# Entry work between the chunks of the last two input slots, and one of four probability tiles scaled on VectorE

## The chip, the cores and the metric

One NeuronCore of a Trainium2 chip runs the kernel. The time is that of the device, in microseconds from the start of the program to its end, taken as the median of several executions. A granted TensorE clock of 1.00 is 2.4 GHz and one of 0.50 is 1.2 GHz.

## The reference, cut to what matters

The program is a stack of two "first" layers (a feed-forward, a mixer with latent attention and convolution, a second feed-forward, a gated embedding) and then one "second" block. The change lies in the mixer of the second block, for 512 tokens and a width of 1024:

```python
z = h @ w_in                                  # 19 slots of 128 columns here
g_rnn, x_rnn, q, k_c, v_c, k_s, v_s, k_w, v_w, gate_logits = jnp.split(z, splits, axis=-1)
...
kc = compress_blocks(to_heads(k_c), ...)      # 31 compressed blocks of keys, and vc of values
...
p_c = jax.nn.softmax(sc, axis=-1) * ...       # scores against the 31 blocks
o_c = jnp.einsum('bgrqc,bgcd->bgrqd', p_c, vc)
...
p_s = jax.nn.softmax(ss...)                   # all blocks are selected at 512 tokens
o_s = jnp.einsum('bgrqnk,bgqnkd->bgrqd', p_s, v_sel)
...
o_w = jnp.einsum('bgrqk,bgkd->bgrqd', jax.nn.softmax(sw, axis=-1), vwb)
return gb[0] * o_c + gb[1] * o_s + gb[2] * o_w
```

So there are three attentions with a common query: one against 31 compressed blocks, and two (called `s` and `w`) that are causal over the tokens. Each is multiplied by a gate, and the gate is folded into the reciprocal of the softmax sum. The multiplication of the probabilities by that number is what the change divides between two engines.

## The kernel before, in words

Everything is fp32, each large product made of three matmuls of split operands (a high and a low part each). The engines run in parallel from orders written out by hand, one straight list for each engine, and meet at counting semaphores. TensorE is called PE, VectorE DVE, ScalarE ACT and GpSimd POOL.

**Input slots.** A weight slot is 128 output columns by the full depth of 1024. `slot_mm` (L1132) works through its 8 chunks of depth (k = 0 to 7), 3 matmuls each, into one of 4 PSUM banks `proj[0..3]`, slot number modulo 4. DVE then takes the bank out (L2054 for slots 15 to 18, which are the queries). DVE also makes the low part of the weights of a slot two slots ahead (L1581, `w_lo`), after ACT has made the high part (L652). Slot 18 is the last.

**Entry.** Between slots 17 and 18 PE does the entry work of the attention (L1428 to L1455): 8 transposes of the two value tensors into `sc` (L1433), 2 of the compressed hidden layer (L1438), the first score pair `scores2(0, 0)` (L1351), the compressed keys and values (L1445 and L1450) and `scores2(0, 1)`. On DVE the partners of these stand in the iteration for slot 17: the hidden layer (L2105, L2106), the gates (L2110), the copies of the turned values (L2115), the hidden columns (L2117), then the first softmax step. After slot 18 come `scores2(1, ...)` and `compressed()` (L1331, 32 matmuls of only 31 columns), which needs slot 18's queries.

**Steps.** The attention has 16 steps g. Four steps make one head pair: 128 queries each, against 512, 384, 256 and 128 keys. A step has four score tiles i (two attentions by two head groups). DVE takes the scores from PSUM, adds the bias and finds the maximum in `biased(g, i)` (L1991); ACT exponentiates and sums (L914); `gated(g)` on DVE makes the reciprocal (L1997) and multiplies it by the gate (L2000); POOL multiplies the four probability tiles by it in `scale(g)` (L623); PE turns them three steps later (`turn2`, L1362) into three PSUM banks in rotation; ACT and DVE take turns at copying these out (`copy_2`, L992 and L2168). So a turn needs the copy of the turn three before it. After four steps `values` (L1375, L1380) multiplies a head pair's turned probabilities by the values, and `take2` on DVE (L2172) copies the result.

**The low parts of the recurrent branch** (`u_lo`, L2179, 4 tiles) stand on DVE between `gated(1)` and the compressed scores. Their reader is the output projection (L1487) after the attention.

## Time and profile before

| | us |
|---|---|
| median of 3 runs | 3057.77 (3054.81 to 3058.88) |
| the profiled execution | 3060.09, span 3058.3 |
| mean granted TensorE clock over the span | 0.989 |
| PE busy | 3001.4 (98%) |
| DVE, ACT, POOL busy | 1699.3, 1109.3, 319.0 |

The span is cut by the profiler from the first to the last instruction; the time of an execution holds some 1.8 us more. Busy times of PE come from pipelined matmuls with modelled ends, so PE can read as busy while it goes at half its clock or below its best rate. The stage that the change touches lies between 2527 and 2639 us from the start.

### The profile page before, as it was taken

To read this page: it belongs to the slowest core of one execution; us is meant where nothing else is said; L and a number is where in the kernel's file an instruction comes from. 1 tells how busy PE (TensorE), PEld (TensorE's weight loads), DVE (VectorE), ACT (ScalarE), POOL (GpSimd) and SP (SyncE) were. 2 spreads that over 40 slices of the span, in tenths; PEclk is the share of its full clock that TensorE was granted. 3 is DMA by queue.
4 is the path that set the end of the run, shared out by engine and by line. 5 is a ranking of instruction groups with operands and counts; after the bars stand their busy time and mean duration, and the time that the engine had idled before them with its cause. 6 is when DMAs were issued, how large, how long until landed. Compare 5 with 4: busy or idle time off the path is not lost. (4 is left out here: it accounts for less than half of the span.)

```text
span 3058.3 us, 37437 instructions
## 1 busy us (share of the span) xinstructions
PE 3001.4 (98%) x13534; PEld 2437.9 (80%) x13534; DVE 1699.3 (56%) x2387; ACT 1109.3 (36%) x1724; POOL 319.0 (10%) x254
## 2 busy tenths in 40 slices
PE   7999999999999999999999999999999999989999
PEld 6888888778888887888888888888888775678887
DVE  6555565565654556555456455655546677453334
ACT  4222333562332234322232454332324555552223
POOL 1000200000100024000030000200003216500000
PEclk9999999999999999999999999999999998999999
DMA  5242222123323222432222212343222420122222
GB/s 186 87 151 96 90 96 83 57 61 114 138 96 144 97 79 94 147 138 100 91 99 92 84 37 88 107 144 138 97 93 83 158 76 22 42 70 97 96 96 82
DMA packets 86809, 301.58 MB, mean 99 GB/s; under 512 B 10272, under 2 KB 19616, under 8 KB 85536
## 3 DMA queue, kind: packets, MB, share of 16 engines
q1 hardware_dynamic: 86688, 300.02, 28.6%
q8 instruction: 70, 1.15, 0.1%
q14 instruction: 51, 0.42, 0.0%
HBM read 297.88 MB, written 2.10 MB: 98 GB/s over the span
## 5 line engine op out<-in xcount | busy, mean ns | idle before, releaser
L1128 PE MATMUL proj<-u_hi,w_hi 128*128 128x512 f32 x2616 | 1029.9, 394 | 28.3 <-DVE u_lo L1586 22.0
L1130 PE MATMUL proj<-u_hi,w_lo 128*128 128x512 f32 x2616 | 1021.8, 391 | 0.0
L1129 PE MATMUL proj<-u_lo,w_hi 128*128 128x512 f32 x2616 | 1021.6, 391 | 0.0
L1581 DVE TENSOR_TENSOR w_lo<-raw,w_hi 128x1024 fp32r<-128x1024 f32 (+4 forms) x567 | 656.7, 1161 | 492.6 <-ACT w_hi L652 483.2
L652 ACT ACTIVATE w_hi<-raw 128x1024 fp32r<-128x1024 f32 (+4 forms) x567 | 536.2, 954 | 342.2 <-PE proj L1130 220.3
L1128 PEld LDWEIGHTS proj<-u_hi,w_hi 128*128 128x128 f32 x2616 | 493.0, 188 | 141.5 <-issue 23.5
L1129 PEld LDWEIGHTS proj<-u_lo,w_hi 128*128 128x128 f32 x2616 | 493.2, 189 | 103.4 <-issue 2.9
L1130 PEld LDWEIGHTS proj<-u_hi,w_lo 128*128 128x128 f32 x2616 | 492.8, 188 | 103.2
L1128 PE MATMUL proj<-a_hi,w_hi 128*128 128x512 f32 x936 | 368.4, 394 | 3.1 <-DVE w_lo L1581 1.5
L1130 PE MATMUL proj<-a_hi,w_lo 128*128 128x512 f32 x936 | 365.2, 390 | 0.0
L1129 PE MATMUL proj<-a_lo,w_hi 128*128 128x512 f32 x936 | 364.8, 390 | 0.0
L1597 DVE TENSOR_TENSOR work<-proj,rs 128x512 f32<-128x512 f32 x260 | 179.4, 690 | 286.8 <-PE proj L1130 286.6
L694 ACT ACTIVATE a_hi<-work 128x512 f32 (+1 forms) x88 | 55.6, 632 | 441.3 <-DVE work L1652 441.3
L1128 PEld LDWEIGHTS proj<-a_hi,w_hi 128*128 128x128 f32 x936 | 175.9, 188 | 42.1 <-DVE a_lo L1655 2.6
L1130 PEld LDWEIGHTS proj<-a_hi,w_lo 128*128 128x128 f32 x936 | 175.7, 188 | 37.1
L1129 PEld LDWEIGHTS proj<-a_lo,w_hi 128*128 128x128 f32 x936 | 176.0, 188 | 34.3
L549 POOL TENSOR_TENSOR acc<-h 128x512 f32<-128x512 f32 x6 | 6.2, 1040 | 1519.3 <-DVE h L1670 1320.1
L1670 DVE SCALAR_TENSOR_TENSOR h<-proj,h 128x512 f32<-128x512 f32 x96 | 66.3, 691 | 165.8 <-PE proj L1130 165.7
L691 ACT ACTIVATE work<-work 128x512 f32<-128x512 f32 x88 | 55.6, 632 | 267.7 <-DVE work L1597 267.7
L1655 DVE TENSOR_TENSOR a_lo<-work,a_hi 128x512 f32 (+1 forms) x88 | 61.0, 693 | 80.4 <-ACT a_hi L694 80.4
L658 ACT ACTIVATE u_hi<-h,vec 128x512 fp32r<-128x512 f32 x48 | 34.8, 724 | 141.1 <-DVE h L1670 82.2
L552 POOL TENSOR_TENSOR sq<-h 128x512 f32<-128x512 f32 x42 | 62.1, 1478 | 72.5 <-DVE h L1918 40.0
(459 smaller groups left out, 2922.4 us busy)
## 6 DMA issues: line engine op xcount, KB each, us to landing
raw<-in_ffn_gu SPq DMA_DIRECT2D x174, 512.0 KB, 3.3
raw<-in_in_w SPq DMA_DIRECT2D x68, 512.0 KB, 3.2
raw<-in_ffn_dn SPq DMA_DIRECT2D x64, 512.0 KB, 3.2
raw<-in_ff SPq DMA_DIRECT2D x64, 512.0 KB, 3.3
gate<-in_ada SPq DMA_DIRECT2D x8, 3072.0 KB, 11.4
raw<-in_ffn_dn SPq DMA_DIRECT2D x32, 384.0 KB, 3.0
raw<-in_in SPq DMA_DIRECT2D x18, 512.0 KB, 3.4
raw<-in_mla_out SPq DMA_DIRECT2D x16, 512.0 KB, 3.3
```

Source lines behind the costliest of these rows:

```text
L552: pool.tensor_tensor(sq, x(m), x(m), ALU.mult).then_inc(sq_ready, 1)
L652: act.activation(wt(w_hi, slot, slot.tiles), wt(raw, slot, slot.tiles), ACT.Copy)\
L658: act.activation(u_hi(m), h(m), ACT.Copy, scale=gain[:, m:m + 1]).then_inc(u_hi_ready, 1)
L691: act.activation(work(2 + q), work(q), ACT.Tanh, scale=0.5).then_inc(tanh_ready, 1)
L694: act.activation(a_hi_t[:, bass.ds((2 * it + q) * S, S)], work(8 + q), ACT.Copy)\
L1128: pe.matmul(out, w_h, x_h, start=first, stop=False)
L1129: pe.matmul(out, w_h, x_l, start=False, stop=False)
L1130: return pe.matmul(out, w_l, x_h, start=False, stop=last)
L1581: dve.tensor_tensor(wt(w_lo, slot, slot.tiles), wt(raw, slot, slot.tiles), wt(w_hi, slot, slot.tiles).bitcast(F32), ALU.subtract).then_inc ...
L1597: return dve.tensor_tensor(dst, proj[:, slot.pos, :], rs, ALU.mult)
L1655: dve.tensor_tensor(a_lo_t[:, at], work(8 + q), a_hi_t[:, at].bitcast(F32), ALU.subtract)\
L1670: dve.scalar_tensor_tensor(at, proj[:, slot.pos, :], 0.25, at, ALU.mult, ALU.add)\
```

## The change

PE's entry work goes between the chunks of slots 17 and 18: at chunk 3 of slot 17 the 8 transposes, now into the banks `proj[3]` and `proj[0]`; at chunk 4 of slot 18 the first score pair and the 2 transposes; at chunk 6 the compressed keys and values and the second score pair. DVE's copies of the turned values move ahead of taking out slot 17. In each step DVE scales tile 0 itself, right behind `gated`, and POOL the other three; the one counter `p2_ready` becomes `p2_pool` and `p2_dve`. The four `u_lo` tiles move from behind `gated(1)` to the loop pass g = 16 (STEPS), ahead of a `take2` and of the last copies.

```diff
--- before.py
+++ after.py
@@ -255,8 +255,9 @@
         dist_ready, hid_part = sem("dist_ready"), sem("hid_part")
         cs_done, cs_exp, pc_step, pc_ready = (sem(n) for n in ("cs_done", "cs_exp", "pc_step", "pc_ready"))
         cs_sub = sem("cs_sub")
-        s2_done, max2, exp2, inv2 = sem("s2_done"), sem("max2"), sem("exp2"), sem("inv2")
-        ginv2, p2_ready, t2_done, o2_done, o2_ready = (sem(n) for n in ("ginv2", "p2_ready", "t2_done", "o2_done", "o2_ready"))
+        s2_done, max2, exp2 = sem("s2_done"), sem("max2"), sem("exp2")
+        ginv2, t2_done, o2_done, o2_ready = (sem(n) for n in ("ginv2", "t2_done", "o2_done", "o2_ready"))
+        p2_pool, p2_dve = sem("p2_pool"), sem("p2_dve")
         pt_act, pt_dve = sem("pt_act"), sem("pt_dve")
         h_turned, h_copied, h_sized = sem("h_turned"), sem("h_copied"), sem("h_sized")
         gain_diag, gain_rows = sem("gain_diag"), sem("gain_rows")
@@ -362,6 +363,7 @@
         t_bank = lambda n: (tr[:, :], proj[:, 2, :], proj[:, 3, :])[n % 3]
         turn_no = lambda g, i: 4 * g + i + (2 if g >= 2 else 0)
         TURN_C = 8
+        scaled = lambda g, i: (p2_pool, 3 * g + i) if i else (p2_dve, g + 1)
         by_act = lambda n: n % 2 == 0
         copied = lambda n: (pt_act if by_act(n) else pt_dve, n // 2 + 1)
 
@@ -619,8 +621,8 @@
             def scale(g):
 
                 pool.wait_ge(ginv2, g + 1)
-                for i in range(4):
-                    pool.tensor_scalar(prob(g, i), prob(g, i), esum(g, i), None, ALU.mult).then_inc(p2_ready, 1)
+                for i in range(1, 4):
+                    pool.tensor_scalar(prob(g, i), prob(g, i), esum(g, i), None, ALU.mult).then_inc(p2_pool, 1)
 
             for g in range(2):
                 scale(g)
@@ -1353,7 +1355,7 @@
 
             def turn2(g, i):
                 n = turn_no(g, i)
-                pe.wait_ge(p2_ready, 4 * g + i + 1)
+                pe.wait_ge(*scaled(g, i))
                 if n >= 3:
                     pe.wait_ge(*copied(n - 3))
                 elif n:
@@ -1382,11 +1384,46 @@
                         if br and k == QT - 1:
                             mm.then_inc(o2_done, 1)
 
+            def beside_17(k):
+
+                if k == 3:
+                    pe.wait_ge(slot_read, Slot(L2, 16).done)
+                    for bank, v in ((3, VS), (0, VW)):
+                        for t in range(QT):
+                            mm = pe.transpose(proj[:, bank, t * P:(t + 1) * P], v[:, t * P:(t + 1) * P], ident[:, :])
+                        mm.then_inc(v2_turned, 1)
+
+            def beside_18(k):
+
+                if k == 4:
+                    pe.wait_ge(h_copied, KD + 3)
+                    scores2(0, 0)
+                    pe.wait_ge(hid_ready, 1)
+                    pe.wait_ge(g_cols, 1)
+                    for m in range(2):
+                        mm = pe.transpose(tr[:, m * P:(m + 1) * P], hid_x[:, m * P:(m + 1) * P], ident[:, :])
+                    mm.then_inc(hid_turned, 1)
+                if k == 6:
+                    pe.wait_ge(hid_cols, 1)
+                    pe.wait_ge(v2_copied, 2)
+                    for m in range(2):
+                        pe.matmul(tr[:, 0:62], w2k(m), hid(0, m), start=m == 0, stop=m == 1)
+                    for g in range(2):
+                        for m in range(2):
+
+                            for c in range(0, P, 32):
+                                mm = pe.matmul(proj[c:c + N_CMP, 3, g * 64:(g + 1) * 64],
+                                               hid(1, m)[:, g * N_CMP:(g + 1) * N_CMP], w2v(m),
+                                               start=m == 0 and g == 0, stop=m == 1, skip_group_check=True)
+                    mm.then_inc(kv_cmp_done, 1)
+                    pe.wait_ge(slot_read, Slot(L2, 17).done)
+                    scores2(0, 1)
+
             for s in range(IN2):
                 if s == 0:
                     two_slots((Slot(L2, 0), Slot(L2, 1)), u_of, lambda k: pe.wait_ge(u_ready, 8 * KD + k + 1))
                 elif s > 1:
-                    slot_mm(Slot(L2, s), u_of)
+                    slot_mm(Slot(L2, s), u_of, {17: beside_17, 18: beside_18}.get(s))
                 if 5 <= s <= 8:
 
                     j = s - 5
@@ -1425,35 +1462,6 @@
                     for t in range(QT):
                         mm = pe.transpose(tr[:, t * P:(t + 1) * P], gT[:, t * P:(t + 1) * P], ident[:, :])
                     mm.then_inc(g_turned, 1)
-                if s == 17:
-
-                    pe.wait_ge(h_copied, KD + 3)
-                    for i, v in enumerate((VS, VW)):
-                        for t in range(QT):
-                            mm = pe.transpose(sc[:, i, t * P:(t + 1) * P], v[:, t * P:(t + 1) * P], ident[:, :])
-                        mm.then_inc(v2_turned, 1)
-                    pe.wait_ge(hid_ready, 1)
-                    pe.wait_ge(g_cols, 1)
-                    for m in range(2):
-                        mm = pe.transpose(tr[:, m * P:(m + 1) * P], hid_x[:, m * P:(m + 1) * P], ident[:, :])
-                    mm.then_inc(hid_turned, 1)
-                    pe.wait_ge(slot_read, Slot(L2, 15).done)
-                    pe.wait_ge(v2_copied, 2)
-                    scores2(0, 0)
-                    pe.wait_ge(hid_cols, 1)
-                    for m in range(2):
-                        pe.matmul(tr[:, 0:62], w2k(m), hid(0, m), start=m == 0, stop=m == 1)
-                    for g in range(2):
-                        for m in range(2):
-
-                            for c in range(0, P, 32):
-                                mm = pe.matmul(proj[c:c + N_CMP, 3, g * 64:(g + 1) * 64],
-                                               hid(1, m)[:, g * N_CMP:(g + 1) * N_CMP], w2v(m),
-                                               start=m == 0 and g == 0, stop=m == 1, skip_group_check=True)
-                    mm.then_inc(kv_cmp_done, 1)
-                    pe.wait_ge(slot_read, Slot(L2, 17).done)
-                    scores2(0, 1)
-
             scores2(1, 0)
             scores2(1, 1)
             compressed()
@@ -1994,10 +2002,11 @@
             def gated(g):
                 j, qt, w = step(g)
                 dve.wait_ge(exp2, 4 * g + 4)
-                dve.reciprocal(esum(g, 0, 4), esum(g, 0, 4)).then_inc(inv2, 1)
-                dve.wait_ge(inv2, g + 1)
+                link(dve.reciprocal(esum(g, 0, 4), esum(g, 0, 4)))
                 inv = esum(g, 0, 4).rearrange("p (b g) -> p b g", b=2)
                 dve.tensor_tensor(inv, inv, gates4[:, qt, 1:3, :, j], ALU.mult).then_inc(ginv2, 1)
+                dve.wait_ge(ginv2, g + 1)
+                dve.tensor_scalar(prob(g, 0), prob(g, 0), esum(g, 0), None, ALU.mult).then_inc(p2_dve, 1)
 
             def build_blocks(kv, g):
 
@@ -2049,6 +2058,10 @@
                     link(dve.scalar_tensor_tensor(top, poly, 2.0, top, ALU.mult, ALU.add))
 
                     link(dve.tensor_scalar(small2[:, 0:4], top, -4.0, None, ALU.mult))
+                if s == 17:
+                    for i, d in enumerate((vn_s, vn_w)):
+                        dve.wait_ge(v2_turned, i + 1)
+                        dve.tensor_copy(d, proj[:, (3, 0)[i], :]).then_inc(v2_copied, 1)
                 if 15 <= s:
                     dve.wait_ge(slot_done, slot.done)
                     dve.scalar_tensor_tensor(dst[s], proj[:, slot.pos, :], q_scale[:, s - 15:s - 14], rs, ALU.mult, ALU.mult)\
@@ -2110,9 +2123,6 @@
                     dve.tensor_scalar(gcols.rearrange("p (t c) -> p t c", t=QT),
                                       tr[:, :].rearrange("p (t c) -> p t c", t=QT)[:, :, 0:24],
                                       1.0, 0.5, ALU.add, ALU.mult).then_inc(g_cols, 1)
-                    for i, d in enumerate((vn_s, vn_w)):
-                        dve.wait_ge(v2_turned, i + 1)
-                        dve.tensor_copy(d, sc[:, i, :]).then_inc(v2_copied, 1)
                     dve.wait_ge(hid_turned, 1)
                     dve.tensor_copy(hid_c, tr[:, 0:2 * P]).then_inc(hid_cols, 1)
                     dve.wait_ge(dist_ready, 2)
@@ -2174,10 +2184,6 @@
             for i in range(4):
                 biased(1, i)
             gated(1)
-            for j in range(4):
-                dve.wait_ge(u_hi_ready, 9 * KD + j + 1)
-                dve.scalar_tensor_tensor(u_lo(j), gr(j), c2(C_RNN + j), u_hi(j).bitcast(F32), ALU.mult, ALU.subtract)\
-                   .then_inc(u_ready, 1)
             cmp_scores()
             for g in range(2, STEPS + 3):
                 behind = g - 2 if g < 4 else g - 3 if g >= 5 else None
@@ -2193,6 +2199,10 @@
                     biased(g, 3)
                 if behind is not None:
                     copy_2(behind, 3)
+                for j in range(4) if g == STEPS else ():
+                    dve.wait_ge(u_hi_ready, 9 * KD + j + 1)
+                    dve.scalar_tensor_tensor(u_lo(j), gr(j), c2(C_RNN + j), u_hi(j).bitcast(F32), ALU.mult, ALU.subtract)\
+                       .then_inc(u_ready, 1)
                 if g == 2:
                     cmp_norm()
                 if g == 4:
```

PE around slots 17 and 18, in the order of before (`sc`, `tr`, `proj` are PSUM; `ax` holds queries, keys and values; the three rows L1128 to L1130 are one chunk): the entry stands in one piece between two slots.

```order
L1130 MATMUL proj<-u_hi,w_lo 128x512
L1433 MATMUL sc<-ident,ax 128x128 [waits h_copied]
L1433 MATMUL sc<-ident,ax 128x128 x7
L1438 MATMUL tr<-ident,ax 128x128 [waits g_cols,hid_ready]
L1438 MATMUL tr<-ident,ax 128x128
L1351 MATMUL sc<-ax 128x512 [waits v2_copied,slot_read]
L1351 MATMUL sc<-ax 128x512
L1445 MATMUL tr<-acc,sq 128x62 [waits hid_cols]
L1445 MATMUL tr<-acc,sq 128x62
L1450 MATMUL proj<-sq,acc 31x64 x16
L1351 MATMUL proj<-ax 128x512 [waits slot_read]
L1351 MATMUL proj<-ax 128x512
```

PE in the changed kernel, inside slot 18, from the last matmul of chunk 3 on:

```order
L1132 MATMUL proj<-u_hi,w_lo 128x512
L1353 MATMUL sc<-ax 128x512 [waits h_copied]
L1353 MATMUL sc<-ax 128x512
L1404 MATMUL tr<-ident,ax 128x128 [waits g_cols,hid_ready]
L1404 MATMUL tr<-ident,ax 128x128
L1130 MATMUL proj<-u_hi,w_hi 128x512
L1131 MATMUL proj<-u_lo,w_hi 128x512
L1132 MATMUL proj<-u_hi,w_lo 128x512
```

The waits are the same, but chunks of slot 18 now stand ahead of them and between them.

DVE at the end of the attention, before (`gate` takes the turned probabilities; the row of L2172 is `take2(2)`, the two of 2x128 are the copies of step 14):

```order
L1997 RECIPROCAL row_stats<-row_stats 128x4 [waits exp2]
L2000 TENSOR_TENSOR row_stats<-row_stats,rope_table 128x4 [waits inv2]
L2168 COPY gate<-proj 128x3x128 [waits t2_done]
L2168 COPY gate<-tr 128x3x128 [waits t2_done]
L2172 COPY work<-ot 128x512 [waits o2_done]
L2168 COPY gate<-proj 128x2x128 [waits t2_done] x2
```

DVE at the same place in the changed kernel:

```order
L2005 RECIPROCAL row_stats<-row_stats 128x4 [waits exp2]
L2007 TENSOR_TENSOR row_stats<-row_stats,rope_table 128x4 [waits start_step]
L2009 TENSOR_SCALAR work<-work,row_stats 128x128 [waits ginv2]
L2178 COPY gate<-proj 128x3x128 [waits t2_done]
L2178 COPY gate<-tr 128x3x128 [waits t2_done]
L2204 SCALAR_TENSOR_TENSOR u_lo<-ax,col_76,u_hi 128x512 [waits u_hi_ready] x4
L2182 COPY work<-ot 128x512 [waits o2_done]
L2178 COPY gate<-proj 128x2x128 [waits t2_done] x2
```

The four `u_lo` tiles came in ahead of `take2(2)` and of the copies of step 14, and one scale came in behind the product with the gates.

## Rows read from the trace of the kernel before

**Rows 1.** Engines and granted clock by stretch; columns: us, then busy time of each.

```profile
core 0: us, PE busy (x) PEld busy (x) DVE busy (x) ACT busy (x) POOL busy (x), PEclk, DMA share, GB/s
2536.50:2543.30 6.80, 6.01 (x46) 2.81 (x44) 2.42 (x7) 1.52 (x4) 0.00 (x0) 0.50 0.01 2
2553.70:2570.60 16.90, 14.87 (x62) 10.08 (x60) 16.27 (x42) 11.30 (x37) 12.66 (x10) 0.50 0.00 0
2615.10:2621.80 6.70, 6.70 (x25) 2.83 (x22) 0.90 (x7) 0.88 (x4) 6.70 (x6) 0.50 0.00 0
2632.20:2635.50 3.30, 3.30 (x14) 1.28 (x12) 0.00 (x0) 0.00 (x0) 0.00 (x0) 0.50 0.00 0
```

**Rows 2.** Timeline of PE around the entry: start, us, instruction, idle before.

```profile
2527.33 0.48 PE L1128 MATMUL proj<-u_hi,w_hi 128*128 128x512 f32 x1
...
2532.91 1.03 PE L1433 MATMUL sc<-ident,ax 128*128 128x128 f32 x8
2536.22 0.41 PE L1438 MATMUL tr<-ident,ax 128*128 128x128 f32 x2 [2.28 <-DVE rope_table L2110]
2537.42 2.08 PE L1351 MATMUL sc<-ax 64*128 64x512 f32 x4 [0.79 <-DVE ax L2115]
2539.43 1.11 PE L1445 MATMUL tr<-acc,sq 128*128 128x62 f32 x4
...
2541.48 2.04 PE L1351 MATMUL proj<-ax 64*128 64x512 f32 x4
...
2549.13 0.92 PE L1351 MATMUL sc<-ax 64*128 64x384 f32 x4
...
2550.53 4.09 PE L1331 MATMUL proj<-rope_table,ax 64*128 64x31 f32 x64
```

**Rows 3.** Timeline of DVE over the same stretch.

```profile
2533.11 0.75 DVE L2054 SCALAR_TENSOR_TENSOR ax<-proj,q_scale,rs 128x512 f32<-128x512 f32 x1 [0.21 <-PE proj L1130]
...
2536.00 1.28 DVE L2115 COPY ax<-sc 128x512 f32<-128x512 f32 x2
...
2543.55 0.69 DVE L1991 CUSTOM_DVE_ANT_0 work<-proj,work 128x512 f32<-128x512 f32 x1 [2.60 <-PE proj L1351]
...
2546.79 1.29 DVE L1581 TENSOR_TENSOR w_lo<-raw,w_hi 128x1024 fp32r<-128x1024 f32 x1 [0.57 <-ACT w_hi L652]
2549.24 0.75 DVE L2054 SCALAR_TENSOR_TENSOR ax<-proj,q_scale,rs 128x512 f32<-128x512 f32 x1 [1.16 <-PE proj L1130]
...
2553.91 3.29 DVE L2179 SCALAR_TENSOR_TENSOR u_lo<-ax,col,u_hi 128x512 fp32r<-128x512 f32 x4 [0.24 <-ACT u_hi L1002]
2557.13 1.24 DVE L2134 TENSOR_TENSOR ux<-proj,work 128x496 f32<-128x496 f32 x2
```

**Rows 4.** The matmuls of L1331 alone, 0.4 us at each clock.

```profile
2552.40:2552.80 0.40, 0.40 (x12) 0.40 (x10) 1.00 0.00 0
2554.00:2554.40 0.40, 0.40 (x6) 0.40 (x6) 0.50 0.00 0
```

**Rows 5.** Groups of DVE, the same scaling in the first attention: busy, mean ns.

```profile
L1749 DVE TENSOR_SCALAR work<-work,row_stats 128x512 f32<-128x512 f32 x16 | 7.8, 486 | 0.6
L1749 DVE TENSOR_SCALAR work<-work,row_stats 128x384 f32<-128x384 f32 x16 | 6.7, 420 | 0.6
...
L1749 DVE TENSOR_SCALAR work<-work,row_stats 128x128 f32<-128x128 f32 x16 | 4.6, 287 | 0.6
```

**Rows 6.** Timeline of POOL, the starts of two successive head pairs.

```profile
2593.31 12.88 POOL L623 TENSOR_SCALAR work<-work,row_stats 128x512 f32<-128x512 f32 x10 [1.65 <-DVE row_stats L2000]
...
2611.64 12.88 POOL L623 TENSOR_SCALAR work<-work,row_stats 128x512 f32<-128x512 f32 x10 [1.33 <-DVE row_stats L2000]
```

**Rows 7.** Engines in steps 8 to 10, columns as in Rows 1.

```profile
2587.60:2597.30 9.70, 9.37 (x52) 4.71 (x52) 9.57 (x41) 8.84 (x29) 7.94 (x9) 1.00 0.01 3
```

**Rows 8.** Timeline of PE and of DVE at the end of the attention.

```profile
2629.75 0.30 PE L1362 MATMUL proj<-ident,work 128*128 128x128 f32 x1 [0.30 <-DVE gate L2168]
...
2631.80 6.22 PE L1380 MATMUL ot<-gate,ax 128*64 128x512 f32 x32
...
2641.31 2.74 DVE L2212 SCALAR_TENSOR_TENSOR u_lo<-work,col,u_hi 128x512 fp32r<-128x512 f32 x4 [2.53 <-ACT u_hi L1030]
```

## The prediction

> **What bounds the kernel now.** I cut the stretch from 2527 to 2639 us by granted clock first. Four stretches stand at 0.50, which is 1.2 GHz: 6.8, 16.9, 6.7 and 3.3 us long [rows 1]. The first follows a wait of PE, the second follows the compressed scores, the third the thin steps of a head pair, the fourth the last turns. So in this stage a wait costs its length and may cost half of what PE does afterwards.
>
> Next the timeline of PE. Between slots 17 and 18 it runs the entry from 2532.91 and waits 2.28 us for the gates and 0.79 us for the turned values; what follows goes at half clock until about 2543.3. The scores of step 1 start at 2549.13, which is the end of slot 18 [rows 1, 2]. Next the timeline of DVE: it takes out slot 18 at 2549.24, then spends 3.29 us on `u_lo` from 2553.91, so that the compressed scores, which PE has ready at about 2554.6, are taken up only at 2557.13 [rows 2, 3]. Until the end of that stretch at half clock DVE is busy 16.27 of 16.90 us [rows 1] and sets the pace, whatever the clock of PE.
>
> In the later head pairs PE and DVE are both nearly full: 9.37 and 9.57 of 9.70 us in steps 8 to 10 [rows 7]. POOL has 17.0 us of work in each 18.33 us (from 2593.31 to 2611.64, of which it idled 1.33 [rows 6]). It is close to being the bound, but it waits for DVE and not the reverse, and its results are used three steps later.
>
> **Entry on PE.** Slot 17 starts at 2527.33 and takes 5.58 us without the transposes [rows 2]. These read 1.03 us busy, with the overlap at both ends about 0.9, so slot 18 starts at 2533.8. Four chunks are half of 5.5 us: 2536.5. The first score pair took 2.0 at half clock from 2537.42 to 2539.43 [rows 2]; at full clock 1.1, with 0.3 for the two transposes: 2537.9. Does it wait? The transposes wait for the gates, which came 3.1 us after DVE began to take out slot 17 (2533.11 to 2536.22 [rows 2, 3]). Now the two value copies, 1.28 us [rows 3], go ahead of that, from 2533.0 on, so slot 17 is taken out at 2534.2 and the gates are there at 2537.3, before the 2537.6 at which PE asks. The margin is 0.3 us; without it the wait is tenths. Chunks 4 and 5 take 1.4, compressed keys and values 1.0 (2.05 at half clock, 2539.43 to 2541.48), the second score pair 1.1, chunks 6 and 7 1.4: slot 18 ends at about 2543.0 instead of 2549.1. **PE gains 6.1 us there**, about 3.1 in waits and 3 in clock. The entry's new waits stand in front of chunks, but nothing queued behind them is due earlier.
>
> **What of it arrives.** DVE's string from the second score pair to the low weights ran from 2543.55 to 2546.79 [rows 3]. It now starts near 2541.7, so the low weights of slot 20 start at 2544.9, behind the new 0.486 us scale [rows 5], which fits ahead of that; slot 18 is taken out at 2546.2 and its queries are there at 2547.0. PE has then finished the scores of step 1 (1.4 us before, 2549.13 to 2550.53 [rows 2]) since about 2544.6 and waits 2.4 us. That is a new wait as long as the one removed. `compressed()` takes 3.9 us at full clock. Its rate is 12 records in 0.4 us at full clock and 6 at half [rows 4]; the clock fell during it even with no wait before it. With a 2.4 us wait in front I expect the fall inside it, somewhere between 2547 and 2550.4, by the nearest case, the wait of rows 2 where the clock was down 0.3 us after it. So it ends between 2551.5 and 2554.9; I take 2553.2. DVE starts there instead of at 2557.13 because `u_lo` is gone: **gain 3.9 us** (2.2 to 5.6; 6.1 if the clock holds). From here DVE's work sets the pace and carries the gain, less the scale of step 2, 0.4 us (between rows 5's 384 and 128 forms). The return of the clock at 2570.6 may come later relative to the work: 0 to 1.7, I take 0 in the likeliest case.
>
> The page "TensorE: Matmul & The Clock Gate" of the Trainium skill, section "Why this matters for your kernels", blames idle gaps between bursts of matmuls for a fall of the clock. The first fall agrees. The second does not: PE went from the scores at 2549.13 straight into the compressed ones and lost the clock within them [rows 1, 2]. By the rule alone, the thin steps of rival B below would be safe; by the row they are not.
>
> **The scale on DVE.** DVE has the same operation in the first attention at 486, 420 and 287 ns [rows 5]. In a head pair the scales of 128, 512 and 384 columns (those behind `gated` of steps 4m-1, 4m, 4m+1) fall where DVE has 0.13 us of idle in 9.7 [rows 7]: 0.29 + 0.49 + 0.42 = 1.2 us. The fourth falls while PE multiplies the values, when DVE is idle (0.90 busy of 6.7 us in the third stretch [rows 1]). PE is nearly full too, so a little slack is eaten: about 1.0 for each of steps 8 to 10 and 12 to 14, and 0.5 for steps 4 to 6, where DVE waits a little. **Loss 2.5 us** (0.5 to 3.6). POOL loses a quarter of 17.0 us in each head pair, which nobody waits for: 0.
>
> "GPSIMD Engine Reference" of the Trainium skill, section "Key points", says that POOL and VectorE contend for shared SBUF interfaces, in VectorE's two-port modes or with two SBUF inputs. The trace agrees for the latter: four `u_lo` tiles took 3.29 us beside busy POOL and the four of L2212 2.74 beside an idle one [rows 3, 8]. By that ratio, 1.2, the scales would cost 0.2 us more in a head pair.
>
> **The tail.** DVE has at g = 16: the copies of step 13, then `u_lo` x4, `take2(2)`, the copies of step 14. PE's turns of step 15 need the copy of (14, 1); before, PE was already released by a DVE copy there, at 2629.75 after 0.30 us of waiting [rows 8]. So there is no slack: POOL is nearly done, u_lo costs 2.7 us by the row of L2212 [rows 8] to 3.3 [rows 3], and step 15's scale 0.3 sits ahead of it. **Loss 2.9 us** (2.7 to 3.6; nothing if the copies turned out to wait for PE anyway). The last 32 value matmuls took 6.22 us with 3.3 us of half clock inside [rows 1, 8], so about 4.7 at full. After a wait near 3 us they may run almost wholly at half clock: +0.9 (0 to +3). The third stretch at half clock, 6.7 us, costs half of itself, 3.4; it came in one of three head pairs. I leave it in, and it may vanish or double.
>
> **Sum**, against the execution profiled (span 3058.3, its own time 3060.1): -3.9 + 0.4 + 2.5 + 2.9 + 0.9 = +2.8, so 3062.9. That execution lay 2.3 above the median of the three runs, 3057.8; on that footing the forecast is 3060.6, and I give **3060.5 us**.
>
> **Rivals.** What a measurement can tell from no change is 0.2%, 6.1 us: 3051.7 to 3063.9.
> - *A. The entry's gain is spent again by the new DVE work and the tail* (the forecast): 3052 to 3064. Chance 0.58.
> - *B. Slower: the clock.* The added DVE work thins PE's steps, and one more head pair falls to 1.2 GHz: 3060.5 + 3.4, with the late return of the clock (+1.7) about 3065.6. For it: steps 12 to 14 fell with PE waiting only tenths, and a little more idling comes to each pair. It decides once one fall more than before comes. Chance 0.22.
> - *C. Faster: POOL was the late one.* Then three tiles instead of four let PE's turns start earlier, the scales on DVE hide, and the `u_lo` tiles find idle DVE: -3.9 - 3.4 (no third fall) with losses of 0.5 near the tail: about 3051. For it: POOL is 93% busy. Against it: it waits 1.3 to 1.65 us for DVE in each pair, and the end of the turns is released by a DVE copy. Chance 0.15.
> - *D. The clock holds through the compressed scores* and the rest is as in A: 3060.5 - 2.2 = 3058.3. Chance 0.05.
>
> **Range.** 3052 to 3067: from the early end of A with the third fall gone (3060.5 - 1.7 - 1.5 - 3.4 - 0.9 is 3053, and C lies just beyond), to B with the full tail price. By 0.2%: faster 0.18 (C and a little of A), same 0.60, slower 0.22.
>
> **What would show it.** In the new profile: PE without a wait between slots 17 and 18 and slot 18 done 6 us sooner; then a wait of about 2.4 us ahead of the compressed scores, and their rate halving within; DVE at L2144 3 to 5 us earlier; two starts of POOL's 512-column group some 19 us apart instead of 18.3; PE waiting about 3 us for a DVE copy in the last turns. The forecast fails if the copies of step 14 had slack, if DVE was not the pace of steps 8 to 14, or if the falls of the clock come at other places.

## The result, and the profile after

| | median us | range | executions |
|---|---|---|---|
| before | 3056.43 | 3053.78 to 3058.88 | 8 |
| changed | 3064.80 | 3061.01 to 3067.06 | 8 |

The ratio is 1.0025, interval 1.0017 to 1.0034: slower by 5.2 to 10.4 us, most likely 7.6. That is just beyond the 0.2% (6.1 us) under which the forecast counts two times as the same; its figure was 3060.5 and its range ended at 3067. Every execution of the changed kernel was slower than the slowest of before. Of the executions of before that ran beside the experiments below, one stood apart at 3749.35 us with a granted clock of 0.754 and is not counted.

The profiled execution of the changed kernel took 3061.01, 3.8 below its median; that of before took 3060.09, 3.7 above its own. Side by side the two profiles show 1 us and not 8. So the traces are read for the place and the size of each step, and the medians for the sum.

First the page's totals, as the busy times of before stand in its table; then the engines by stretch, columns as in [rows 1].

```profile
span 3059.3 us, 37437 instructions
PE 2999.9 (98%) x13534; PEld 2433.9 (80%) x13534; DVE 1705.7 (56%) x2403; ACT 1109.9 (36%) x1724; POOL 303.9 (10%) x238
```

```profile
core 0: us, PE busy (x) PEld busy (x) DVE busy (x) ACT busy (x) POOL busy (x), PEclk, DMA share, GB/s
2549.20:2556.00 6.80, 6.80 (x42) 5.17 (x41) 5.53 (x10) 5.41 (x11) 5.75 (x5) 0.51 0.00 1
2562.80:2569.70 6.90, 6.67 (x21) 3.47 (x20) 5.40 (x21) 4.60 (x14) 4.24 (x6) 0.52 0.01 2
2593.50:2600.40 6.90, 6.89 (x24) 2.63 (x25) 2.28 (x12) 1.12 (x5) 6.90 (x7) 0.52 0.00 0
2631.10:2637.90 6.80, 6.72 (x23) 2.56 (x25) 0.36 (x2) 0.27 (x1) 0.00 (x0) 0.51 0.01 2
2583.80:2593.50 9.70, 8.75 (x48) 4.72 (x46) 9.49 (x36) 8.30 (x26) 5.70 (x6) 1.00 0.01 3
```

Sixteen scales went from POOL (319.0 to 303.9 us) to DVE (1699.3 to 1705.7). The stage has 27.4 us at half clock here, where before had 33.7 [rows 1]: this execution is not slower because the clock fell more. The last row begins in the same step as [rows 7] and is as long: DVE is as full as it was (9.49 of 9.70 us), while PE fell from 9.37 to 8.75. PE now waits for DVE there.

The timeline of PE, at the entry, in the second head pair and in the tail:

```profile
2536.09 1.13 PE L1353 MATMUL sc<-ax 64*128 64x512 f32 x4
...
2542.53 0.92 PE L1353 MATMUL sc<-ax 64*128 64x384 f32 x4
...
2546.66 4.60 PE L1333 MATMUL proj<-rope_table,ax 64*128 64x31 f32 x64 [2.57 <-DVE ax L2067]
...
2574.41 1.07 PE L1377 MATMUL ot<-ux,rope_table 31*64 31x512 f32 x4 [0.26 <-DVE gate L2178]
...
2590.56 0.30 PE L1364 MATMUL tr<-ident,work 128*128 128x128 f32 x1 [0.54 <-DVE gate L2178]
...
2593.51 1.77 PE L1377 MATMUL ot<-ux,rope_table 31*64 31x512 f32 x4 [0.25 <-DVE gate L2178]
...
2630.42 0.30 PE L1364 MATMUL proj<-ident,work 128*128 128x128 f32 x1 [2.69 <-DVE gate L2178]
...
2631.45 1.97 PE L1377 MATMUL ot<-ux,rope_table 31*64 31x512 f32 x4
2633.36 6.87 PE L1382 MATMUL ot<-gate,ax 128*64 128x512 f32 x32
```

The entry has no wait. Slot 18 is done at 2542.53, where it was 2549.13 [rows 2]; slot 17 began 0.5 sooner in this execution, so 6.1 of the 6.6 are the change's. The compressed scores wait 2.57 us for slot 18's queries (L2067). The tail has a wait of 2.69 us for a copy of DVE where before had 0.30 [rows 8]. The half clock from 2593.50 takes the place of that from 2615.10 before [rows 1], one head pair earlier.

The timeline of DVE, entry and tail:

```profile
2532.30 1.28 DVE L2064 COPY ax<-proj 128x512 f32<-128x512 f32 x2
2533.50 0.74 DVE L2067 SCALAR_TENSOR_TENSOR ax<-proj,q_scale,rs 128x512 f32<-128x512 f32 x1
...
2536.23 0.23 DVE L2123 TENSOR_SCALAR rope_table<-tr 128x96 f32<-128x96 f32 x1
...
2545.78 0.74 DVE L2067 SCALAR_TENSOR_TENSOR ax<-proj,q_scale,rs 128x512 f32<-128x512 f32 x1
...
2551.23 1.26 DVE L2144 TENSOR_TENSOR ux<-proj,work 128x496 f32<-128x496 f32 x2 [0.76 <-PE proj L1333]
...
2625.44 0.29 DVE L2009 TENSOR_SCALAR work<-work,row_stats 128x128 f32<-128x128 f32 x1
...
2626.58 2.76 DVE L2204 SCALAR_TENSOR_TENSOR u_lo<-ax,col,u_hi 128x512 fp32r<-128x512 f32 x4
...
2629.86 0.74 DVE L2178 COPY gate<-proj 128x256 f32<-128x256 f32 x2
```

The compressed scores are taken up (L2144) at 2551.23, where it was 2557.13 [rows 3]: 5.9 sooner, 5.4 without the offset. In the tail the four low parts stand between the copies of step 13 and that of step 14 for which PE waits.

DVE at the end of step 9, first in the kernel before and then in the changed one:

```profile
2595.65 0.17 DVE L2000 TENSOR_TENSOR row_stats<-row_stats,rope_table 128x4 f32<-128x4 f32 x1
2595.73 0.28 DVE L2168 COPY gate<-proj 128x128 f32<-128x128 f32 x1
```

```profile
2592.51 0.17 DVE L2007 TENSOR_TENSOR row_stats<-row_stats,rope_table 128x4 f32<-128x4 f32 x1
2592.71 0.55 DVE L2009 TENSOR_SCALAR work<-work,row_stats 128x384 f32<-128x384 f32 x1
2593.18 0.27 DVE L2178 COPY gate<-proj 128x128 f32<-128x128 f32 x1
```

The copy comes 0.67 us behind the start of the product with the gates, where it came 0.08. The scale takes 0.47 of that, by its start and the next one; the rest it waits for the product, whose counter it needs. In steps 7 and 8 the copy comes 0.40 and 0.60 behind, where it came 0.09 and 0.08. So the three scales cost DVE 1.42 us in a head pair, 1.07 of them the scales themselves.

POOL, for [rows 6], and the new scales on DVE by form, for [rows 5]:

```profile
2589.65 9.61 POOL L625 TENSOR_SCALAR work<-work,row_stats 128x512 f32<-128x512 f32 x7 [2.46 <-DVE row_stats L2007]
...
2612.03 9.62 POOL L625 TENSOR_SCALAR work<-work,row_stats 128x512 f32<-128x512 f32 x7 [2.46 <-DVE row_stats L2007]
```

```profile
L2009 DVE TENSOR_SCALAR work<-work,row_stats 128x256 f32<-128x256 f32 x4 | 2.4, 598 | 0.1
L2009 DVE TENSOR_SCALAR work<-work,row_stats 128x384 f32<-128x384 f32 x4 | 2.1, 520 | 0.1
L2009 DVE TENSOR_SCALAR work<-work,row_stats 128x512 f32<-128x512 f32 x4 | 1.9, 486 | 0.1
...
L2009 DVE TENSOR_SCALAR work<-work,row_stats 128x128 f32<-128x128 f32 x4 | 1.1, 286 | 0.1
```

POOL waits for DVE longer than before, 2.46 us against 1.33 to 1.65, and the timeline of PE shows no wait for POOL in this stage. Its two starts are 22.38 us apart and not some 19, because the half clock from 2593.50 lies between them; without half of its 6.9 us it would be 18.9.

In the kernel before, POOL was late once:

```profile
2574.19 0.41 PE L1362 MATMUL proj<-ident,work 128*128 128x128 f32 x2 [0.74 <-POOL ax L623]
```

With three tiles on POOL (the kernel with the scale alone, below) PE waits 0.99 us at that place, for ACT. So the relief of POOL brought nothing there, and rival C falls.

### The profile page after: what moved, and what is told of

Its sections match the earlier page's. It is cut to its first block and busy times, and to the rows that moved or that the text cites. A ratio compares the mean times of both kernels' runs of the same rounds, so it can differ in the third digit from the quotient of the medians.

```text
span 3059.3 us, 37437 instructions
## 1 busy us (share of the span) xinstructions
PE 2999.9 (98%) x13534; PEld 2433.9 (80%) x13534; DVE 1705.7 (56%) x2403; ACT 1109.9 (36%) x1724; POOL 303.9 (10%) x238
## 5 line engine op out<-in xcount | busy, mean ns | idle before, releaser
L1130 PE MATMUL proj<-u_hi,w_hi 128*128 128x512 f32 x2616 | 1029.3, 393 | 27.3 <-DVE u_lo L1594 20.9
L1130 PEld LDWEIGHTS proj<-u_hi,w_hi 128*128 128x128 f32 x2616 | 492.5, 188 | 140.8 <-issue 22.8
L1131 PEld LDWEIGHTS proj<-u_lo,w_hi 128*128 128x128 f32 x2616 | 493.0, 188 | 103.4 <-issue 2.9
L1130 PE MATMUL proj<-a_hi,w_hi 128*128 128x512 f32 x936 | 368.1, 393 | 3.1 <-DVE w_lo L1589 1.5
L1130 PEld LDWEIGHTS proj<-a_hi,w_hi 128*128 128x128 f32 x936 | 175.8, 188 | 42.1 <-DVE a_lo L1663 2.6
```

Of the source, the lines that this page charges most:

```text
L1130: pe.matmul(out, w_h, x_h, start=first, stop=False)
L1131: pe.matmul(out, w_h, x_l, start=False, stop=False)
```

## Experiments

"Stage" is read from each profile: from the start of slot 17 on PE to the first matmul behind the value matmuls (L1504, before L1496). It is 110.6 us before and 113.4 in the changed kernel. An execution that was early or late when the stage began does not disturb it, but the falls of the clock that this one execution had are in it. Ratios are to before on the same chip, with 11 executions of each kernel and 33 of before. A difference in us is the ratio's; where times fall into groups it can lie some us off that of the medians.

| kernel | median us | ratio, interval | profiled | stage |
|---|---|---|---|---|
| entry alone | 3055.63 | 1.0001 (0.9992 to 1.0010) | 3060.49 | 110.8 |
| scale on DVE alone | 3061.16 | 1.0016 (1.0007 to 1.0025) | 3063.19 | 113.5 |
| low parts moved, alone | 3058.61 | 1.0010 (1.0001 to 1.0019) | 3059.23 | 110.3 |
| changed, low parts back | 3059.52 | 1.0011 (1.0002 to 1.0020) | 3059.52 | 110.1 |
| changed, low parts behind the last copies | 3058.12 | 1.0007 (0.9998 to 1.0016) | 3057.95 | 109.4 |
| entry, low parts behind the last copies | 3055.28 | 0.9997 (0.9988 to 1.0006) | 3057.08 | 107.1 |
| the same, slot 18 out early | 3052.40 | 0.9995 (0.9986 to 1.0004) | 3051.07 | 101.5 |
| one scale in four on DVE | 3053.58 | 0.9986 (0.9977 to 0.9995) | 3048.39 | 100.0 |

**The entry alone.** Of the changed kernel, undone are the move of the low parts and the scale:

```diff
-                for i in range(1, 4):
+                for i in range(4):
                     pool.tensor_scalar(prob(g, i), prob(g, i), esum(g, i), None, ALU.mult).then_inc(p2_pool, 1)
...
             gated(1)
+            for j in range(4):
...
+                dve.scalar_tensor_tensor(u_lo(j), gr(j), c2(C_RNN + j), u_hi(j).bitcast(F32), ALU.mult, ALU.subtract)\
             cmp_scores()
```

> The entry between the chunks alone: POOL scales all four tiles and u_lo stands behind gated(1) as before. My sum: slot 18 done 6 us sooner, but the compressed scores wait some 2.5 us for slot 18's queries and DVE has u_lo in front of them, so DVE takes up the compressed scores 3.5 us sooner than before: about -3.5 us against the kernel before (range -6 to -1). Rival (clock): the new wait moves the fall of the clock into PE-bound work and the entry is worth nothing: 0 or above. Rival (pure gain): -6.

No change, with at most 2.4 us gained by the interval, where 3.5 was expected: a miss. Eight executions lie between 3053.97 and 3055.87 and three between 3060.07 and 3060.49; the profiled one is of the three. The timeline of PE in it:

```profile
2547.17 7.04 PE L1333 MATMUL proj<-rope_table,ax 64*128 64x31 f32 x64 [2.29 <-DVE ax L2065]
```

The compressed scores run wholly at half clock behind their new wait, 7.04 us, where the changed kernel's profile has 4.60 and before 4.09 [rows 2]. In this execution the wait and the clock together take back 2.29 + 2.95 us of what the entry won. The eight faster ones have no trace; their median lies only 1.2 below that of before.

**The scale alone.** In the kernel before:

```diff
-                for i in range(4):
-                    pool.tensor_scalar(prob(g, i), prob(g, i), esum(g, i), None, ALU.mult).then_inc(p2_ready, 1)
+                for i in range(1, 4):
+                    pool.tensor_scalar(prob(g, i), prob(g, i), esum(g, i), None, ALU.mult).then_inc(p2_pool, 1)
...
                 dve.tensor_tensor(inv, inv, gates4[:, qt, 1:3, :, j], ALU.mult).then_inc(ginv2, 1)
+                dve.wait_ge(ginv2, g + 1)
+                dve.tensor_scalar(prob(g, 0), prob(g, 0), esum(g, 0), None, ALU.mult).then_inc(p2_dve, 1)
```

> The first tile's scale on DVE alone, entry and u_lo as before. My sum: +2.9 us (0.4 for step 2, 0.5 and twice 1.0 for the three full head pairs, 0.3 at the end), so +1 to +4. Rival (clock): thinner steps let one more head pair fall to 1.2 GHz in most executions: +6. Rival (POOL was the late one): -1 or below.

Slower by 4.9 us (2.1 to 7.6). PE in its second head pair:

```profile
2580.49 1.07 PE L1377 MATMUL ot<-ux,rope_table 31*64 31x512 f32 x4
2596.65 0.30 PE L1364 MATMUL tr<-ident,work 128*128 128x128 f32 x1 [0.54 <-DVE gate L2171]
...
2599.60 1.94 PE L1377 MATMUL ot<-ux,rope_table 31*64 31x512 f32 x4 [0.26 <-DVE gate L2171]
```

From one value group to the next it takes 19.11 us, where before took 17.93 (2578.39 to 2596.32). The waits of the changed kernel, 0.54 and 0.26 us, are in it, so they come from the scale alone. The forecast's 2.9 lies inside the interval.

**The move of the low parts alone.** In the kernel before, the loop is taken from behind `gated(1)` and put behind `copy_2(behind, 3)` for `g == STEPS`, as in the change's diff.

> The move of the four u_lo tiles to the pass g = 16 alone. My sum: DVE takes up the compressed scores as soon as PE has them, 2.5 us sooner; the last turns wait 2.7 us for the copies of step 14 and the value matmuls after it go longer at half clock, 0.9: about +1.1 us (range -1 to +4). Rival (the tail costs more): the wait in the tail and the clock after it cost 6: +3.5. Rival (the tail is covered): -2.5.

Slower by 3.1 us (0.3 to 5.8), where 1.1 was expected and 3.5 by the rival of a dearer tail. PE and DVE in the tail:

```profile
2627.47 0.30 PE L1362 MATMUL proj<-ident,work 128*128 128x128 f32 x1 [3.02 <-DVE gate L2168]
```

```profile
2622.94 3.45 DVE L2194 SCALAR_TENSOR_TENSOR u_lo<-ax,col,u_hi 128x512 fp32r<-128x512 f32 x4
```

The wait of the tail comes from this part by itself. The three parts alone give +0.3, +4.9 and +3.1, which is 8.3 against the 7.6 of the whole: within their intervals, some 2.7 us either way each, they add up.

**The low parts put back in the changed kernel:** the second half of the diff of the entry alone.

> The changed kernel with u_lo back behind gated(1). The changed kernel measured +8 us against before. My sum: -3.5 for the entry, +2.9 for the scale: -0.6 (range -3 to +3), so the u_lo move would be what makes the changed kernel slower by most of 8. Rival (scale and clock): +4 to +6, nearly as slow as the changed kernel.

Slower than before by 3.4 us (0.6 to 6.1), 4.3 less than the changed kernel. The 0.6 faster that was expected missed by 4.0; the entry alone missed by 3.8. The prediction priced the tail, with its clock, at 3.8; the 4.3 is net of what the low parts cost DVE at the front, where they stand again.

**The low parts behind the last copies:**

```diff
-                for j in range(4) if g == STEPS else ():
+                for j in range(4) if g == STEPS + 2 else ():
```

> The changed kernel with the four u_lo tiles two passes later (g = 18), behind the last copies, where DVE idled 7 us. The changed kernel was +8 against before. If the tail is what u_lo costs there (wait of 2.7 us and half clock after it), this gives back 4 to 5 us: about +3.5 (range +2 to +5). Rival (a wait in the tail is no loss, the rest is clock chance elsewhere): stays above +6.

2.1 us slower than before (-0.6 to 4.9), so this one line gives back 5.5 of 7.6. No wait above 0.30 is left in its tail.

**The entry, with the low parts behind the last copies and four tiles on POOL:**

> Entry between the chunks, u_lo behind the last copies, POOL scales all four tiles. By adding the parts: entry 0, u_lo out of the front -2 to -3 and nothing in the tail, no scale on DVE: -3 (range -5 to 0) against before. Rival (POOL with four tiles becomes the bound once the front is shorter): 0 or above.

0.9 us faster than before (3.7 faster to 1.8 slower), not to be told from it; 3 was expected. Beside the last three kernels it gave 0.9995 (below). Against the kernel above, the scale makes 3.0 of difference.

**The same, slot 18 taken out early,** ahead of `gated(0)` and of the splitting of slot 20's weights:

```diff
                     dve.tensor_copy(vcmp, proj[:, 3, 0:P]).then_inc(kv_cmp_ready, 1)
+                    last = Slot(L2, 18)
+                    dve.wait_ge(slot_done, last.done)
+                    dve.scalar_tensor_tensor(dst[18], proj[:, last.pos, :], q_scale[:, 3:4], rs, ALU.mult, ALU.mult)\
+                       .then_inc(slot_read, 1)
                     gated(0)
```

> As the entry with u_lo at the end and POOL scaling four tiles, and DVE takes slot 18 out ahead of gated(0) and of the split of slot 20. If the wait ahead of the compressed scores (2.3 to 2.6 us) is what eats the entry's gain, by its length and by the clock in those scores (7.0 us instead of 3.9 where it fell at once), it shrinks to under 1 us here and the kernel gains 2 to 5 us more: -5 to -8 against before. Rival (DVE sets the pace behind it anyway, the wait only moves): no more than -1 against the same kernel without it.

```profile
2545.01 3.66 PE L1333 MATMUL proj<-rope_table,ax 64*128 64x31 f32 x64
```

The wait is gone and the compressed scores run at full clock in 3.66 us. Yet the ratio is only 0.9995 (1.5 us faster, -1.2 to 4.3), where 5 to 8 was expected: a miss. Its times fall into two groups, six from 3051.07 to 3052.40 and five from 3057.45 to 3058.30; the median falls into the first and lies 4.7 below that of before, which by itself would overstate the gain. The profiled execution is the fastest of all, and even there the clock fell at 2551.0, in the steps behind, for 17 us. So the fall that was in the scores came later. What the slower group has in its place, no trace shows.

**The first tile on DVE only where DVE is free.** In the changed kernel with the low parts behind the last copies, DVE scales in steps 2, 6, 10 and 14. In the last three of these `gated` falls beside the value matmuls (step 2 stands ahead of the first of them); POOL does all four tiles in the others:

```diff
+        on_dve = lambda g: g % 4 == 2
...
-                for i in range(1, 4):
+                for i in range(on_dve(g), 4):
...
+                if on_dve(g):
+                    dve.wait_ge(ginv2, g + 1)
+                    dve.tensor_scalar(prob(g, 0), prob(g, 0), esum(g, 0), None, ALU.mult).then_inc(p2_dve, 1)
```

> As the changed kernel with u_lo at the end, but DVE scales tile 0 only in steps 2, 6, 10 and 14, whose scale falls where PE multiplies the values and DVE idles; POOL scales the rest. If the scale costs by DVE's time in its full stretches, this costs under 0.5 us: equal to the kernel in which POOL scales all (about -3). Rival (any scale on DVE, by the shared interface or by the added wait, costs in proportion to its number): a quarter of +4.9 above it.

Faster than before by 4.3 us (1.5 to 7.0); about 3 was expected. PE:

```profile
2571.97 1.07 PE L1378 MATMUL ot<-ux,rope_table 31*64 31x512 f32 x4
...
2589.91 1.07 PE L1378 MATMUL ot<-ux,rope_table 31*64 31x512 f32 x4
...
2620.41 0.33 PE L1365 MATMUL proj<-ident,ax 128*128 128x128 f32 x1 [0.25 <-POOL ax L626]
```

The pair takes 17.94 us again: a scale that lies beside the value matmuls costs nothing, although it is the slowest form (598 ns in the mean, above).

**Four kernels on one chip.** The last three, and the one with both the early slot 18 and the hidden scale:

| kernel | median us | range | ratio, interval | stage |
|---|---|---|---|---|
| entry, low parts at the end | 3056.03 | 3052.05 to 3056.77 | 0.9995 (0.9986 to 1.0004) | 103.6 |
| + slot 18 early | 3054.30 | 3051.22 to 3058.14 | 0.9994 (0.9985 to 1.0003) | 103.4 |
| + one scale in four on DVE | 3053.55 | 3047.01 to 3055.23 | 0.9983 (0.9974 to 0.9992) | 105.3 |
| + both | 3049.88 | 3048.39 to 3052.20 | 0.9977 (0.9968 to 0.9986) | 101.9 |

> The entry between the chunks, slot 18 taken out early, the low weights behind the last copies, and the first tile scaled on DVE only in steps 2, 6, 10 and 14. If the sum of terms holds (the scale costs nothing where PE multiplies values, the early queries remove the 2.5 us wait ahead of the compressed scores), it is the fastest of the four: 6 to 8 us below before, pitch of the value matmuls 17.9 to 18.4 us, no wait ahead of the compressed scores. If the falls of the clock alone decide (rival), the early queries give nothing on top: 2 to 5 us below before, the fast end as of the kernel without them, the long stretch at half clock from about 2551 present.

> The entry between the chunks and the low weights behind the last copies, all four tiles on GpSimd, once more, beside the others on one chip. Sum of terms: 1 to 3 us below before, 3 to 5 above the kernel with both the hidden scale and the early queries. Rival (GpSimd late in the tail costs something): 1 us or more above the kernel with the hidden scale.

> The same with slot 18 taken out early, once more. Sum of terms: 2 to 4 us below the kernel without it, 4 to 6 below before. Rival (the clock takes back what the early queries give): the same as without it within 1 us, in two groups of times some 6 us apart.

> The entry between the chunks, the low weights behind the last copies, the first tile on DVE only in steps 2, 6, 10 and 14, once more. If a scale beside the value matmuls costs nothing and gives nothing: as with all four tiles on GpSimd, within 1 us, 1 to 3 below before. If it frees the tail from GpSimd: 1 to 3 us below the kernel with four tiles on GpSimd, 3 to 5 below before.

Against before, the kernel with both, the one with the hidden scale and the one with neither came within 0.2 us of what was expected: 6 to 8, 3 to 5 and 1 to 3 faster, measured 7.0, 5.2 and 1.5. The early slot 18 alone missed its 4 to 6 with 1.8 and met its rival: as without it, with times in groups. With both, the kernel is faster than before by 7.0 us (4.3 to 9.8), and each of its executions is faster than any of the changed kernel. PE in it:

```profile
2544.21 3.66 PE L1334 MATMUL proj<-rope_table,ax 64*128 64x31 f32 x64
...
2550.46 1.09 PE L1365 MATMUL proj<-ident,work 128*128 128x128 f32 x4 [1.36 <-DVE ux L2150]
...
2622.57 0.30 PE L1365 MATMUL proj<-ident,work 128*128 128x128 f32 x1 [0.30 <-DVE gate L2184]
...
2624.57 4.53 PE L1383 MATMUL ot<-gate,ax 128*64 128x512 f32 x32
2629.02 1.05 PE L1505 MATMUL sc<-ones,ax 128*128 128x1 f32 x8
```

The tail has no wait above 0.30, and the 32 value matmuls take 4.53 us at full clock, where before took 6.22. The sign of the rival is there too: the clock fell at 2548.7, behind the scores, for 10.2 us. With four tiles on POOL the tail reads otherwise (the first of these four kernels):

```profile
2621.04 0.44 PE L1364 MATMUL proj<-ident,ux 128*128 128x128 f32 x2 [0.45 <-POOL ux L625]
2622.21 0.33 PE L1364 MATMUL tr<-ident,ax 128*128 128x128 f32 x1 [0.25 <-POOL ax L625]
```

There PE waits four times for POOL, 1.2 us in all: 0.45, and three of 0.25. So once the low parts are out of the tail, POOL is the late one at the last turns, and the tile of step 14 taken from it pays. That explains 0.9 us: from the third value group to the fourth it takes 14.34 us with four tiles and 13.42 with the hidden scale, both from profiles with no half clock in that stretch. The ratios differ by 3.7 us (and by 5.2 with slot 18 early). What the rest is, the runs do not settle.

## Why the prediction was nearly right, and what was off

The range held and so did the direction, but not the size: from the executions it went by, the forecast was some 3 us slower, and the change made it 7.6.

- *The entry's order: right.* No wait in it, slot 18 done 6.1 us sooner as forecast, and a new wait of 2.57 where 2.4 stood.
- *The gain that arrives, 3.9 (2.2 to 5.6): 5.4 in one trace, near nothing in the time.* The profiled execution kept full clock up to 2549.2, so it lay at the good end. Its first value group began 3.4 us sooner, net of the offset (forecast 3.9 less 0.4 and 0.5, so 3.0). Of the 5.4, then, 2.0 were gone again by there; PE had a new wait of 1.91 us for a copy of ACT at 2561.03, which the forecast did not have. But the part alone gave 0.3 slower (3.1 slower to 2.4 faster), and its profile, like that of the kernel with the low parts put back, had 7.04 us of compressed scores. This is the term that was mis-sized: I let the clock fall somewhere within the scores; of the eight profiles that have that wait, five have the scores at 6.89 or 7.04 us, that is at half clock from their start, and three at 4.23, 4.60 and 5.29. And where the wait was taken away, a fall behind the scores took its place. Why the clock falls at one place or the other stays open.
- *The scale on DVE, 2.5 + 0.4: right in mechanism, a little small.* The scales of steps 7 to 9 take 0.20, 0.40 and 0.47 us of DVE by the starts, 1.1 in all where 1.2 stood. The sum had nothing for DVE's wait for its own product ahead of each, which makes it 1.4. The delay is 1.17 us a pair where 1.0 stood, and PE's waits for DVE copies (0.54 and 0.25) are its visible part. Alone it cost 4.9 (2.1 to 7.6), within the changed kernel about 3.0.
- *The tail, 2.9: right; its half clock, 0.9 (0 to 3): 1.5.* The wait is 2.69 for 0.30, `u_lo` 2.76, the value groups behind it 1.97 and 6.87 for 1.07 and 6.22. Undone, it gives back 4.3, and 5.5 when the low parts stand behind everything.
- *POOL: nothing gained, as forecast.* It only waits longer. Rival C (0.15) needed it late. It was so once in the kernel before, for 0.74 us, where PE waits for ACT once POOL is relieved; otherwise only at the last turns, 1.2 us at most.
- *Rival B (0.22)* had nearly the measured time, 3065.6, by another mechanism: one fall of the clock more. The changed kernel's profile does not show it: one fall from the first value group to the fourth, as before, and although the tail's grew from 3.3 to 6.8 us, less half clock in sum. But that execution was the fastest of the eight, and two other kernels with a scale on DVE in every step do have one fall more there. The scale alone, and then the changed kernel with the low parts put back:

```profile
2623.60:2627.00 3.40, 3.40 (x17) 1.31 (x14) 0.86 (x3) 0.00 (x0) 3.40 (x4) 0.50 0.00 0
2619.90:2623.30 3.40, 3.40 (x16) 1.43 (x12) 0.98 (x3) 0.00 (x0) 3.40 (x4) 0.50 0.00 0
```

Each stands beside a fall of 6.8 us in the pair ahead. The four profiles of such kernels hold 6.8 or 10.2 us at half clock between those value groups, the ten others 0 to 6.8. So B had something for it, which with one profile of each kernel is not shown; if it is so in most executions, half of those 3.4 us would be near the 2.0 by which the scale alone cost more than forecast (an estimate).
- *Rival D (0.05)* needed full clock through the compressed scores, and came only once slot 18 was taken out early.
- *The sum.* By the trace it is right to a tenth: the stage is 2.7 us longer, and +2.8 was forecast. By value groups, with the fall that came one pair earlier set off, the front is 3.4 shorter, the two pairs 1.8 longer, the last turns 2.8 and the matmuls behind them 1.5, against 3.0, 2.0, 2.9 and 0.9. That the profiled execution, the fastest of the eight, fits so well is in part luck: the others were slower by up to 6. The medians differ by 8.4. I took off 2.3 for where the profiled execution of before lay to its median and left the changed kernel to lie as far above its own; it lay 3.8 below. Against the parts alone, each forecast was too fast: the entry by 3.8, the scale by 2.0 and the low parts by 2.0 us. Only the first lies outside its interval, so of the 4.3 us by which 3060.5 missed the median, the entry's gain is the part that is shown.

## What to carry to other kernels

Work taken from an engine for which nobody waits and given to the one that sets the pace costs about its full length, however short the instruction is there: 1.1 us of scales and 0.3 of waiting on a DVE that was 99% busy became 1.17 us a head pair, and the same instruction beside the value matmuls cost nothing. Low-priority work that is put off must go behind the last thing anyone waits for, not ahead of it: two iterations later it gave back 5.5 of 7.6 us. An early finish on one engine can be worth nothing where its successor waits for another engine: slot 18 was done 6.1 us sooner, and the entry alone gained nothing that could be told. And where a few us of half clock come and go, judge by medians of many executions, since two profiles here showed 1 us of a difference of 8.

## What the runs showed of the hardware that was not expected

- The falls of the clock follow the waits loosely. With slot 18 early, the wait of 2.3 us was gone and the clock held through the compressed scores, but in the three profiles of that kind it fell 2.3, 1.7 and 0.8 us behind them, for 17.1, 10.2 and 10.2 us. The times of one kernel split into groups some 4 to 6 us apart (the entry alone: 3053.97 to 3055.87, and 3060.07 to 3060.49).
- Most of the distance between two such groups can be half clock. The kernel with the hidden scale was profiled on two chips, once in each of its groups, at 3048.39 and 3054.78 us. The compressed scores in the two:

```profile
2546.31 5.29 PE L1334 MATMUL proj<-rope_table,ax 64*128 64x31 f32 x64 [2.28 <-DVE ax L2069]
2547.53 6.89 PE L1334 MATMUL proj<-rope_table,ax 64*128 64x31 f32 x64 [2.29 <-DVE ax L2069]
```

The stage holds 10.2 us at half clock in the first and 20.4 in the second; half of the difference is 5.1, and the stage is 5.3 us longer.
- A scale on DVE took 354 ns for 256 columns in the first attention and 598 here, the 384 form 420 [rows 5] and 520; the 128 and 512 forms stayed at 286 and 486. In the second pair the 512 form began at 2589.59, just ahead of POOL's start at 2589.65, and took 0.48; the 384 form at 2592.71 and the 256 form at 2595.37 lay within POOL's 9.61 us and took 0.55 and 0.68. In step 2 the 256 form began at 2562.24, again just ahead of POOL's start at 2562.31, and took 0.35. "GPSIMD Engine Reference" of the Trainium skill, section "Key points", says that the two engines contend for shared SBUF interfaces when VectorE is in a two-port mode or reads two SBUF inputs. The trace agrees that they contend; the scale reads one tile, so by the page it would be the mode, which no row here shows. My forecast put this at 0.2 us a pair; it did not decide, since the slowest form lies where DVE is free.
